# The first mixer reordered: recurrence preparation beside the attention heads, the token shift in four column groups, and attention's end inside the first tile's levels

## The reference, cut to what the change touches

The program is one block of a model over 256 tokens of width 1024. Its first stage is a mixer with two halves that read the same projection `w_in`: attention with a forget gate ("fox", 8 heads of 64) and a recurrence with a low-rank decay ("rw", 8 heads of 64). Everything after the mixer (a second mixer, experts, cross attention, a feed-forward part) is as before.

## Time and profile before

| | us |
|---|---|
| median of 3 runs | 1717.57 (1715.75 to 1718.66) |
| the profiled execution | 1712.33 |
| its span in the trace | 1710.2 |
| PE busy in the span | 1402.2 |
| DVE busy | 680.0 |
| ACT busy | 389.6 |
| POOL busy | 110.7 |

### The profile page before, as it was taken

How to read it: one execution, slowest core, us unless ns; L and a number is a source line. 1 busy time by engine, 2 the same in 40 slices (tenths; PEclk the granted TensorE clock), 3 DMA queues, 4 the chain that set the end, 5 groups by cost and what they waited for, 6 DMA issues and landing times.

```text
span 1710.2 us, 17757 instructions
## 1 busy us (share of the span) xinstructions
PE 1402.2 (82%) x6756; PEld 880.7 (51%) x6756; DVE 680.0 (40%) x1203; ACT 389.6 (23%) x617; POOL 110.7 (6%) x37
## 2 busy tenths in 40 slices
PE   3876823778896899999999999589868767599996
PEld 1433511667754444444444444466546436399974
DVE  2005257544447222222222222463265522467652
ACT  0101123310001122221222221244221011344442
POOL 0100183730000000000000000000000000000000
PEclk8988955598987899999999999699859987799998
DMA  9732122430145299999999997544411121155451
GB/s 337 228 116 82 35 83 99 152 119 1 50 165 237 119 402 421 411 422 414 415 418 417 412 414 299 198 153 142 83 41 50 49 99 49 49 166 166 166 171 71
DMA packets 98397, 338.69 MB, mean 198 GB/s; under 512 B 13664, under 2 KB 39683, under 8 KB 69545
## 3 DMA queue, kind: packets, MB, share of 16 engines
q1 hardware_dynamic: 84162, 319.08, 48.6%
q10 hardware_dynamic: 9528, 15.46, 3.2%
q0 software_dynamic: 4656, 3.44, 0.9%
HBM read 332.94 MB, written 1.05 MB: 195 GB/s over the span
## 4 chain that ended last, share of the span: by engine, by line
PE 69%; DVE 14%; issue 10%; DMA 2%; ACT 2%; POOL 2%; ACTq 1%; DVEq 0%; POOLq 0%
PE bank L1579 14%; PE bank L1595 7%; PE bank L1204 6%; PE bank L1223 6%; PE bank L1225 5%; PE bank L1224 5%; PE bank L1542 2%; PE bank L1235 2%; PE bank L1543 2%; PE bank L1403 2%; PE bank L1560 2%; PE bank L1562 2%; PE bank L1693 2%; DMA c_triu<-const_triu 1%; PE bank L1407 1%
## 5 line engine op out<-in xcount | busy, mean ns | idle before, releaser
L1204 PE MATMUL bank<-ring,xT 128*128 128x512 f32 (+3 forms) x480 | 196.8, 564 | 18.5 <-DMA ring<-in_w_in 12.6
L1204 PEld LDWEIGHTS bank<-ring,xT 128*128 128x128 f32 x480 | 91.8, 207 | 113.9 <-issue 93.2
L1595 PE MATMUL bank<-dn,tmp 128*64 128x512 f32 x528 | 120.6, 598 | 0.0
L1223 PE MATMUL bank<-mod,w_high 128*128 128x256 f32 x352 | 100.9, 287 | 11.4 <-PE bank L1225 5.4
L2478 DVE TENSOR_TENSOR xT<-bank,mod 128x512 fp32r<-128x512 f32 x66 | 45.6, 691 | 158.0 <-ACT mod L981 150.7
L2471 DVE SCALAR_TENSOR_TENSOR tmp<-silu_c,rc,bank 128x256 f32<-128x256 f32 x33 | 22.6, 684 | 196.8 <-ACT silu_c L968 191.4
L1224 PE MATMUL bank<-xT,w_high 128*128 128x256 f32 x352 | 99.2, 282 | 0.0
L1225 PE MATMUL bank<-mod,ring 128*128 128x256 f32 x352 | 98.8, 281 | 0.0
L2841 DVE TENSOR_TENSOR ring<-ring,w_high 128x1024 fp32r<-128x1024 f32 x66 | 77.7, 1220 | 26.2 <-ACT w_high L1146 24.6
L1235 PE MATMUL bank<-c_ident,xn 128*128 128x128 f32 x120 | 28.0, 412 | 69.3 <-DVEq L2541 25.4
L1973 POOL TENSOR_TENSOR ring<-ring 128x2048 f32<-128x2048 f32 x16 | 72.5, 4536 | 42.7 <-ACT ring L880 42.1
(11 more groups left out here) (581 smaller groups left out, 2538.8 us busy)
## 6 DMA issues: line engine op xcount, KB each, us to landing
dn<-in_exp_w_down SPq DMA_DIRECT2D x66, 1024.0 KB, 10.3
ring<-in_exp_w_gate SPq DMA_DIRECT2D x34, 1024.0 KB, 9.7
ring<-in_exp_w_up SPq DMA_DIRECT2D x34, 1024.0 KB, 11.8
gu_odd<-in_exp_w_gate SPq DMA_DIRECT2D x32, 1024.0 KB, 9.9
gu_odd<-in_exp_w_up SPq DMA_DIRECT2D x32, 1024.0 KB, 12.0
ring<-in_w_ffn_in SPq DMA_DIRECT2D x22, 1024.0 KB, 5.1
ring<-in_ada_w SPq DMA_DIRECT2D x16, 1024.0 KB, 4.9
ring<-in_w_in SPq DMA_DIRECT2D x7, 2048.0 KB, 18.8
```

Of the source, the lines that this page charges most:

```text
L1204: mm = pe.matmul(bank[lin_bank(o)][:, 0:n], lhs(k, t), ring[:, j % RING, k * n:(k + 1) * n], start=(k == 0), stop=(k == kt - 1 and not bias))
L1223: pe.matmul(out, w[0], x[0], start=start, stop=False, skip_group_check=True)
L1595: mm = pe.matmul(bank[6 + h][CHUNKS[c], :], act_eT[:, 0, k, CHUNKS[c]], dn[:, 2 * parity + c, lo:lo + BANK], start=(k == 0), stop=(k == D_ ...
```

The core of the diff, in the order jobs, ACT, POOL, DVE:

```diff
-        FOX_JOBS = [(512, 512), (1024, 512), (2048, 24), (0, 512), (1536, 512)]
-        RW_JOBS = [(FOX_COLS, 512), (FOX_COLS + 512, 512), (FOX_COLS + 1024, 512), (FOX_COLS + 1536, 288)]
-        for lo, n in FOX_JOBS + RW_JOBS:
+        IN_JOBS = [(512, 512), (1024, 512), (2048, 24), (0, 512),
+                   (FOX_COLS + 1536, 288), (FOX_COLS, 512), (FOX_COLS + 512, 512), (FOX_COLS + 1024, 512), (1536, 512)]
+        J_K, J_V, J_FG, J_Q, J_LORA, J_R, J_KR, J_VR, J_G = range(len(IN_JOBS))
...
+            for j in range(RING):
+                act.wait_ge(w_full[j], 16)
...
+            for j in (J_Q, J_LORA):
+                for t in range(T):
+                    in_copy(j, t)
             rstd(fs[:, 6, 0:16], fs[:, 5, 0:16])
             rstd(fs[:, 8, 0:16], fs[:, 7, 0:16])
             for t in range(T):
-                side_copy(J_RW + 1, t)
...
+                in_copy(J_R, t)
+            act.wait_ge(lerp_done, 1)
+            act.activation(z_rw[:, :, 1536:1600], z_rw[:, :, 1536:1600], ACT.Tanh)
...
+                if h in (1, 2):
+                    in_copy(J_VR, h - 1)
+                elif h in (3, 4):
+                    in_copy(J_G, h - 3)
+                    low_rank_sigmoids(h - 3)
...
+            scale_late(2)
             rstd(fs[:, 6, 0:16], fs[:, 5, 0:16])
...
+            scale_late(LATE_UNITS - 6)
...
+                if t == 0:
+                    scale_late(4)
...
+            for i, j in enumerate((J_LORA, J_R, J_KR, J_VR)):
+                lo, width = IN_JOBS[j]
+                lo -= FOX_COLS
+                prev, z = z_prev[:, i % 2, :, 0:width], z_rw[:, :, lo:lo + width]
+                pool.wait_ge(lin_evac, after(j, 1))
+                link(pool.memset(prev[0:1, 0, :], 0.0))
+                pool.dma_start(prev[1:P, :, :], z[0:P - 1, :, :]).then_inc(zr_shifted, 16)
+                pool.dma_start(prev[0:1, 1, :], z[P - 1:P, 0, :]).then_inc(zr_shifted, 16)
+                pool.wait_ge(zr_shifted, 32 * (i + 1))
+                link(pool.tensor_tensor(prev, prev, z, ALU.subtract))
+                link(pool.tensor_tensor(prev, prev, mu[:, lo:lo + width].unsqueeze(1).broadcast_to([P, T, width]), ALU.mult))
+                link(pool.tensor_tensor(z, z, prev, ALU.add))
+                pool.sem_inc(lerp_done, 1)
             pool.wait_ge(w_used, J_OUT)
             pool.memset(ada_sums, 0.0).then_inc(late_zero, 1)
-            pool.wait_ge(lin_evac, after(J_RW + 3, 1))
-            pool.wait_ge(par_loaded, 16 * 16)
-            for i, t in enumerate((1, 0)):
-                pool.dma_start(z_prev[1:P, :], z_rw[0:P - 1, t, :]).then_inc(zr_shifted, 16)
...
+            masked_scores(3)
+            low_rank_sums(0)
+            prob_copy(2)
+            key_norms()
+            masked_scores(4)
+            low_rank_sums(1)
+            prob_copy(3)
+            masked_scores(5)
+            for t in range(T):
+                log_decay(t)
+            prob_copy(4)
+            keys_and_bonus(0)
+            masked_scores(6)
+            prob_copy(5)
+            keys_and_bonus(1)
+            shifted_decay(0)
+            masked_scores(7)
+            prob_copy(6)
+            decayed(0)
+            prob_copy(7)
+            shifted_decay(1)
+            decayed(1)
+            dve.wait_ge(lerp_done, 4)
...
+                    if t == 0 and level == 1:
+                        head_outputs()
+                    elif t == 0 and 2 <= level <= 3:
+                        head_gates(level - 2)
```

More of the change, by code:

```diff
@@ L217, in build @@
-        k_aug = sb("k_aug", [P, T, HEADS, AUG], fox_stack)
+        with ExitStack() as before_heads:
+            kv_prev = sb("kv_prev", [P, T, 2 * W1], before_heads)
+            q_aug = sb("q_aug", [P, T, HEADS, AUG], before_heads)
+            k_aug = sb("k_aug", [P, T, HEADS, AUG], before_heads)
+        logw = sb("logw", [P, T, W1], side_stack)
+        iclr = sb("iclr", [P, T, W1], side_stack)
+        gate = sb("gate", [P, T, W1], side_stack)
+        y_rw = sb("y_rw", [P, T, W1], side_stack)
@@ L219, in build @@
         prT = xn[:, :, W1:W1 + 3 * P]
[L220 to L230, removed]
@@ L1342, in _, with decay_sums @@
                     .then_inc(sc_mm, 1)
-            pe.wait_ge(const1_loaded, 16 * len(CONST_1))
-            for t in range(T):
+            def decay_sums(t):
+                pe.wait_ge(const1_loaded, 16 * len(CONST_1))
                 pe.wait_ge(logw_ready, t + 1)
@@ L2110, in prob_copy, with masked_scores @@
                 dve.tensor_copy(prT[:, h % 2, :], bank[4 + g % 2][:, 0:3 * P]).then_inc(tp_evac, 1)
-            dve.wait_ge(const1_loaded, 16 * len(CONST_1))
-            for h in range(HEADS):
-                n = SC_FOX + h
+            R = lambda t: z_rw[:, t, 0:W1]
+            K = lambda t: z_rw[:, t, W1:2 * W1]
+            def masked_scores(h):
+                n = SC_FOX[h]
                 dve.wait_ge(sc_mm, n + 1)
@@ L2153, in _, with low_rank_sums @@
                     .then_inc(tp_evac, 1)
-            for t in range(T):
-                n = SC_LORA + 3 * t
+            def low_rank_sums(t):
+                n = SC_LORA[t]
                 b = lambda i: bank[6 + (n + i) % 2][:, :]
@@ new lines, in _ @@
+            prob_copy(1)
+            masked_scores(3)
[6 more added lines that the diff above has]
+            masked_scores(5)
+            for t in range(T):
+                log_decay(t)
[6 more added lines that the diff above has]
+            masked_scores(7)
@@ L2210, in _, with head_outputs @@
+            prob_copy(6)
[4 more added lines that the diff above has]
+            dve.wait_ge(lerp_done, 4)
             dve.wait_ge(rw_exp, 5)
             dve.sem_inc(sc_evac, 1)
+            def head_outputs():
+                dve.wait_ge(prob_ready, HEADS)
+                link(dve.reciprocal(fs[:, 11, 0:16], fs[:, 10, 0:16]))
+                dve.wait_ge(pv_mm, HEADS)
+                inv_sum = fs[:, 11, 0:16].rearrange("p (h t) -> p t h", t=T)
+                for t in range(T):
+                    o = xn[:, t, 0:W1]
+                    link(dve.tensor_tensor(heads(o), heads(bank[2 + t][:, :]), per_head(inv_sum[:, t, :]), ALU.mult))
+                    link(dve.tensor_tensor(head_sq, o, o, ALU.mult))
+                    link(dve.tensor_reduce(fs[:, 5, 8 * t:8 * t + 8], heads(head_sq), AX.X, ALU.add))
+                dve.sem_inc(pv_evac, 1)
+                link(dve.tensor_scalar(fs[:, 5, 0:16], fs[:, 5, 0:16], 1.0 / HD, RMS_EPS, ALU.mult, ALU.add))
+                dve.reciprocal(fs[:, 5, 0:16], fs[:, 5, 0:16]).then_inc(inv_var, 1)
+                rstd_n[0] += 1
```

346 lines of the change are left out of this document (175 added, 171 removed).

## The result

The changed kernel takes 1724.72 us (median of 20 runs, 1712.95 to 1729.16) against 1716.93 for the kernel before in the same series (1712.42 to 1721.29): 7.8 us more. The kernel is slower, by little. The forecast was 1720.7 in a range from 1704 to 1734, and the sum +3.1. The profiled execution takes 1728.36 us with a span of 1726.4.

What follows compares the result with a forecast made beforehand. It took DVE and POOL work laid end to end between attention's end and tile 0 as the bound there, with PE and DVE alternating in the levels. Terms: -13.9 + 12.0 + 5 = +3.1, so 1720.7 us, range 1704 to 1734.

Steps and rivals of the forecast that it cites:

- The early edits: Before the shift: an earlier `c_triu` transfer may start K's job sooner; 4 us less to 2 more, taken as 0.
- Term 1: Token shift until KR is shifted: one-engine transfers, R 31.5 and KR 26.5 us; KR's lerp ends at 229.2, bounds 215 to 239.
- Term 2: From KR's lerp end to tile 0's start: 58 us of work and waits, so tile 0 starts at 287.2, 13.9 earlier.
- Term 3: Tile 0's levels, with `head_outputs` and gates added on DVE, hits and lower PE clock: 12.0 us longer, bounds 3 to 17.
- The price of a hit: DVE gate operation held by POOL adding a late unit: 4.41 instead of 0.69 us, so 3.7 lost each.
- The ACT queue: ACT's ten late units ahead of tile 0's first copy: free at 89 us, PE asks at 93, hidden by 4 us.
- Term 4: Tile 1's level 0, with the last four late units added over it: at most two hits of 3.7, taken as 5 us.
- The direction: Whole kernel against the one before: slower 0.42, faster 0.31, same 0.27.
- The spread transfers: Rival on the shift transfers: spread over the engines, KR ready by 190, tile 0 37 us earlier, total 1697; chance 0.13.
- The rival in which ACT becomes what PE waits for: Tile 0 pays more: all gates hit, ACT's late units slower; +18 there, +7 behind, 1729, or 1734; chance 0.21.

## Why the prediction was right

**The early edits, taken as 0.** V's job starts at 54.41 instead of 55.13, though K's started 2.9 us earlier; ACT's copies of K did not come before 53.67, behind the parameter loads. Right.

**Term 1, KR ready at 229.2.** Measured 232.1. R's two copies end at 153.1, not 156.7, since `kv_prev` landed at 135.29 instead of 139.56: "Nothing in the change moves that" was wrong, by 3.6 us in our favour. The transfers took 34.0 and 28.6 us, where I had 31.5 and 26.5 for them, and clearing, gaps and operations 1.8 more than worked out. What comes on top of the 20.0 us is 8.6 for KR, not 6.5, and 9.0 for R beside the 5.0 of the weight load: mis-sized by 2.1 and 2.5. The four errors leave 2.9. That the new form goes through one engine was the step on which all rested, and it was shown by its opposite: the same bytes in rows of one dimension took 4.3 us and the whole kernel 30 us less.

**Term 2, 58 us from there to tile 0.** Measured 62.1, so the start came at 294.2 instead of 287.2 and the gain was 6.9 instead of 13.9. This is the term that was off by most. I had the output gate's tile beside head 4 at 7.03; after the long wait PE begins it at its lower clock (0.50 from 240 to 248, 0.74 over the row) and takes 9.47, and DVE waits 10.3 instead of 7.7 behind it. POOL's VR lerp holds three operations, not two, for 5.9 us instead of 4.4. PE's row:

```profile
247.99 9.47 PE L1221 MATMUL bank<-ring,xT 128*128 128x512 f32 x16
```

**Term 3, tile 0 longer by 12.0.** Measured 14.7. The holding was 5.0 as taken, on two of the six gate operations. The clock cost 3 x 2.54 = 7.6 instead of 5.4: a level at the lower clock costs more than the 1.8 that I read from the first level before, because that level was already partly at the higher one (its wait for PE was 4.81, where a level behind a gap has 5.58 now). Against this, the changed kernel's first level no longer pays the 1.8, which I had not taken off, so the clock is 5.8 net. The rest of the 2.7 is in the main 0.6 less saved in level 0 and 1.4 behind the last mask, which I had not counted and which is PE's clock again.

The price of a hit was read from a wrong scene. The last gate before, 4.41 us at 235.39, was not held while POOL added a late unit; those additions begin at 248.02. POOL was in the token shift then:

```profile
235.23 4.02 POOL L1959 TENSOR_TENSOR z_prev<-z_prev,z_rw 128x1824 f32<-128x1824 f32 x1 [4.07 <-DMA z_prev<-z_rw]
```

That the price of 3.7 also held for late units is borne out by the 4.88 of the changed kernel. And the lower bound of 3 for this term was added up wrongly: without hits and clock the terms named give 1.6.

The ACT queue had the 4 us of slack that was worked out (3.47), and it became the bound as soon as anything took more than that out of the levels.

**Term 4, tile 1 longer by 5.** Measured 4.2 to its result and 1.5 behind it.

**The sum.** +3.1 forecast, +13.5 at the mixer's end of the profile: +7.0 from term 2 and start, +2.7 from term 3, +0.7 from term 4 and the end. The medians differ by 7.8. The mechanism was right: one engine for the transfers, the wait ahead of the key norms, the lower clock behind the gaps, POOL's hits. The direction was too, but it was only the likeliest of three at 0.42. The size was not: against the medians the sum is 4.7 short, against the mixer's end in the profiles 10, and against the spans 13. That 1720.7 lies within 4 us of the measured median is in part luck, since the sum was worked out from a trace and the trace gives more.

**What stays open.** All three profiles of the changed kernel, 1728.4 to 1733.1 us, lie at the upper end of its 20 runs or above it, and its runs spread over 16 us, where the kernel before has 9. The traced part of the mixer does not vary, and what follows it varies by 4.8 us with PE's clock. In all traces of the changed kernel and its variants that part takes 1188.7 to 1194.7 us, longer than the 1187.2 before, although nothing in it was changed. Whether the short runs have only a higher clock there or a shorter mixer too is not shown: no profile of one of them is at hand.

**The rivals.** The spread transfers were forecast at 1697 and 20 us below the kernel before; made so, they gave 1694.3 and 22. The rival in which ACT becomes what PE waits for did not come about in the changed kernel, but did in the experiments that shortened what lies ahead of ACT's late units, until these were moved too.

## What to carry to other kernels

Before a shift between partitions is cut into groups, look at the pattern of its transfer: one of 127x2x512 went through one engine at 26 GB/s here and was usable after some 29 us, where two of 127x512 with the same bytes were usable after 4.3. In a chain that gates a list of work on another engine this cost 26.5 us of DVE's wait and 30 us of the kernel. When work is moved into a tight loop between two engines, count with it the clock that the idle one loses (2.5 us a level here) and the third engine that may hold the operations (up to 4.4 us each), and ask which queue stands just behind: the gain that one edit takes out of the loop is lost there until both are moved. Late, unhurried work of POOL was not free here: it held DVE operations with two operands in SBUF and copies of a constant, while those that read a bank kept their 0.69 us. It wants a stretch of the program without such operations.

## What the runs showed that I had not expected

- The profile's figure from issue to landing is no measure for a transfer on one engine. For the four transfers `z_prev<-z_rw` of the changed kernel it gives 8.2 to 9.6 us, while POOL's wait for them ended 28 to 36 us after the issue. (The 36 is the low-rank group's, which stood behind `kv_prev` on the same queue; split in two it still took 34, to 137.00, with `kv_prev` in use from 136.25, so this group says nothing about its form.) The small transfer queued behind says more (24.9 us in the median).
- Of the additions that POOL makes, how many hit depends on ACT's order more than on their number: with the same sixteen, 10.0 us of DVE were held in the changed kernel and 30.9 with attention's end placed first.
- The issue itself costs by the pattern: 3.68 us of POOL for 127x2x512, and 1.10 for two of 127x512. And the large one is cut up otherwise: in the window of KR's transfer, 197 to 225 us, 1953 of 2080 packets are under 512 B, and for about four microseconds behind the issue the DMA engines are 20 to 30% busy at 4 to 22 GB/s before the 26 GB/s of one engine set in. With the issue that is most of the 8.6 us on top. The split pair has 192 packets, 64 of them under 512 B.
